# Rotary embedding of retention: how the exchanged key and query tiles are made

## The reference, cut to what matters

```
def axial_rope(x, row, col):
    def rot(xa, pos):
        half = xa.shape[-1] // 2
        freqs = ROPE_BASE ** (-jnp.arange(half, dtype=jnp.float32) / half)
        ang = pos.astype(jnp.float32)[:, None] * freqs[None, :]
        ...
        x1, x2 = xa[..., :half], xa[..., half:]
        return jnp.concatenate([x1 * cos - x2 * sin, x1 * sin + x2 * cos], axis=-1)
    h = x.shape[-1] // 2
    return jnp.concatenate([rot(x[..., :h], row), rot(x[..., h:], col)], axis=-1)
```

## Time and profile before

| | us |
|---|---|
| median of 3 runs | 2415.36 (2414.86 to 2416.98) |
| the profiled execution, its own time | 2415.04 |
| its span, first to last instruction | 2413.2 |
| PE busy | 2363.9 (98%) |
| DVE busy | 1605.0 (67%) |
| ACT busy | 930.6 (39%) |

### The profile page before, as it was taken

One profiled execution on the slowest core, in us unless ns is written; L12 is line 12 of the kernel. 1 busy time (PEld: TensorE's weight loads), 2 busy tenths in 40 slices (PEclk: granted clock), 3 DMA queues, 4 the chain that ended last, 5 costly groups with the idle time before them and its releaser, 6 DMA issues.

```text
span 2413.2 us, 33085 instructions
## 1 busy us (share of the span) xinstructions
PE 2363.9 (98%) x13282; PEld 2040.7 (85%) x13282; DVE 1605.0 (67%) x2128; ACT 930.6 (39%) x1373; POOL 125.5 (5%) x158
## 2 busy tenths in 40 slices
PE   7999999999999999999999999999999999999998
PEld 4888988998877888898889888889889896997996
DVE  7567658856368545686666786676688556678656
ACT  3422346442126322352224464224455324544343
POOL 1000001101100000010000010000010010000000
PEclk9999999999999999999999999999999999999999
DMA  9555555651233344544456575446556343675763
GB/s 298 165 163 179 189 195 162 183 183 62 55 111 88 123 131 129 159 138 151 159 173 200 175 221 162 157 162 203 185 181 183 102 129 110 216 253 185 223 203 123
DMA packets 466444, 396.33 MB, mean 164 GB/s; under 512 B 34148, under 2 KB 418292, under 8 KB 466036
## 3 DMA queue, kind: packets, MB, share of 16 engines
q1 hardware_dynamic: 450704, 386.98, 51.0%
q10 hardware_dynamic: 15588, 7.23, 1.2%
HBM read 392.99 MB, written 1.17 MB: 163 GB/s over the span
## 4 chain that ended last, share of the span: by engine, by line
PE 87%; DVE 9%; ACT 2%; issue 2%; DMA 1%; POOL 0%; SPq 0%; DVEq 0%; ACTq 0%
PE ps L1549 26%; PE ps L1551 26%; PE ps L1550 26%; DVE wl L955 2%; PE ps L1816 1%; PE ps L1892 1%; DVE st L1023 1%; PE ps L1871 1%; PE ps L1985 1%; PE ps L1596 1%; ACT wh L568 1%; PE ps L1797 1%; ACT tB L588 1%; DVE tA L1095 1%; PE ps L1631 1%
## 5 line engine op out<-in xcount | busy, mean ns | idle before, releaser
L955 DVE TENSOR_TENSOR wl<-raw,wh 128x1024 fp32r<-128x1024 f32 x560 | 681.2, 1220 | 587.0 <-ACT wh L568 585.6
L568 ACT ACTIVATE wh<-raw 128x1024 fp32r<-128x1024 f32 x560 | 592.0, 1059 | 1203.1 <-PE ps L1551 1135.3
L1549 PE MATMUL ps<-hh,wh 128*128 128x256 f32 (+1 forms) x2736 | 892.9, 326 | 8.5 <-DVE hl L1109 5.7
L1550 PE MATMUL ps<-hl,wh 128*128 128x256 f32 (+1 forms) x2736 | 885.3, 324 | 0.0
L1551 PE MATMUL ps<-hh,wl 128*128 128x256 f32 (+1 forms) x2736 | 885.1, 324 | 0.0
L1549 PEld LDWEIGHTS ps<-hh,wh 128*128 128x128 f32 x2736 | 520.9, 190 | 55.5 <-DVE hl L1109 7.6
L1550 PEld LDWEIGHTS ps<-hl,wh 128*128 128x128 f32 x2736 | 521.0, 190 | 41.7 <-issue 1.0
L1551 PEld LDWEIGHTS ps<-hh,wl 128*128 128x128 f32 x2736 | 521.0, 190 | 40.7
L970 DVE SCALAR_TENSOR_TENSOR acc<-araw,c,acc 128x1024 f32<-128x1024 f32 x210 | 258.7, 1279 | 58.0 <-DMA araw<-in_ada_w 56.1
L1549 PE MATMUL ps<-wh,stage_h_f 128*128 128x512 f32 x616 | 240.7, 391 | 2.0 <-DVE stage_l_f L1191 2.0
L1551 PE MATMUL ps<-wh,stage_l_f 128*128 128x512 f32 x616 | 239.8, 389 | 0.0
(11 more groups left out here) (187 smaller groups left out, 2277.9 us busy)
## 6 DMA issues: line engine op xcount, KB each, us to landing
raw<-in_ffa_w SPq DMA_DIRECT2D x204, 512.0 KB, 3.9
raw<-in_ffb_w SPq DMA_DIRECT2D x168, 512.0 KB, 3.8
raw<-in_mix_w_in SPq DMA_DIRECT2D x148, 512.0 KB, 4.2
araw<-in_ada_w SPq DMA_DIRECT2D x136, 512.0 KB, 5.1
raw<-in_ret_w_out SPq DMA_DIRECT2D x16, 512.0 KB, 4.5
raw<-in_na_fou_w_out SPq DMA_DIRECT2D x16, 512.0 KB, 4.0
raw<-in_mix_w_o SPq DMA_DIRECT2D x16, 512.0 KB, 3.5
raw<-in_ada_w SPq DMA_DIRECT2D x8, 512.0 KB, 5.2
```

The lines of the kernel that those rows point to most:

```text
L568: A.activation(w_home(u)[0], raw[:, s, :], ACT.Copy).then_inc(w_rounded, 1)
L955: V.tensor_tensor(low, raw[:, s, :], f(high), ALU.subtract).then_inc(w_split, 1)
L1549: T.matmul(out, a[0], b[0], start=start, stop=False)
L1550: T.matmul(out, a[0], b[1], start=False, stop=False)
```

## The change

PE's products with the swap matrix go, with the matrix, its load and their slots in PE's list. In their place ACT copies the four blocks of 32 partitions of a tile, crosswise, into a buffer (`rq2[:, j % 2, 1]`, two of them in turn). The signs move into the sine table. DVE's three operations stay, but the first reads the copied tile from SBUF instead of PSUM, and they stand two units later (after unit 12 + j instead of 10 + j). The constants are loaded one step earlier from that point on, one fewer. The bank of a unit is now n mod 4 instead of its slot mod 4.

```
+ROPE_0, ROPE_LAG = KD, 4
 def ret_slots(l):
-        if KD + 2 <= n < KD + 10:
-            out.append(("rope", j, ret_steps(l)[n - 2][0] - KD))
+        if ROPE_0 + ROPE_LAG <= n < ROPE_0 + ROPE_LAG + 8:
+            out.append(("rope", j, ret_steps(l)[n - ROPE_LAG][0] - KD))
...
 # ACT
+            def rope_swap(l, j):
+
+                n, quarter = ROPE_0 + j, DK // 4
+                t, to = kq[:, ret_steps(l)[n][0] - KD, 0:SEQ], rq2[:, j % 2, 1]
+                act.wait_ge(in_copied, 4 + in0[l] + n + 1)
+                if j >= 2:
+                    act.wait_ge(rope_done, 8 * l + j - 1)
+                for a in range(4):
+                    b = a ^ 1
+                    ins = A.copy(to[a * quarter:(a + 1) * quarter], t[b * quarter:(b + 1) * quarter])
+                ins.then_inc(rope_swapped, 1)
...
                 for j in range(RET[l]):
                     rounded(u + 4 + j)
+                    if ROPE_0 + 2 <= j < ROPE_0 + 10:
+                        rope_swap(l, j - ROPE_0 - 2)
...
 # DVE
-            def rope(l, j, k, bank):
+            def rope(l, j, k):
                 t = kq[:, k, 0:SEQ]
-                dve.wait_ge(rope_mm, 8 * l + j + 1)
-                V.tensor_tensor(rq2[:, j % 2, 0], ps[:, bank, 0:SEQ], ropeS[:], ALU.mult)
+                dve.wait_ge(rope_swapped, 8 * l + j + 1)
+                V.tensor_tensor(rq2[:, j % 2, 0], rq2[:, j % 2, 1], ropeS[:], ALU.mult)
                 link(V.tensor_tensor(t, t, ropeC[:], ALU.mult))
                 V.tensor_tensor(t, t, rq2[:, j % 2, 0], ALU.add).then_inc(rope_done, 1)
...
 # PE
-                for m, slot in enumerate(slots):
-                    if m >= 4:
-                        before = slots[m - 4]
-                        if before[0] == "unit":
-                            pe.wait_ge(in_copied, c0 + 3 + before[1] + 1)
-                        else:
-                            pe.wait_ge(rope_done, 8 * l + before[1] + 1)
-                    if slot[0] == "rope":
-                        _, j, k = slot
-                        pe.wait_ge(in_copied, c0 + 3 + KD + j + 1)
-                        T.matmul(ps[:, B[m % 4], 0:SEQ], swap[:], kq[:, k, 0:SEQ], start=True, stop=True).then_inc(rope_mm, 1)
-                        continue
-                    _, n, r, lo, hi = slot
+                for n, (r, lo, hi) in enumerate(ret_steps(l)):
+                    if n >= 4:
+                        pe.wait_ge(in_copied, c0 + 3 + n - 3)
...
-                    form_a(u + n, B[m % 4], src, hi, n0=lo)
+                    form_a(u + n, B[n % 4], src, hi, n0=lo)
...
 # constants
+        S[half * 2 * q:half * 2 * q + q] *= -1
```

More of the change, by code:

```diff
@@ L134, in trunk @@
         ident = sb("ident", [P, P])
-        swap = sb("swap", [P, P])
         ropeC = sb("ropeC", [P, SEQ])
@@ L237, in trunk @@
         rg_sig, rg_silu = sem("rg_sig"), sem("rg_silu")
-        rope_mm, rope_done = sem("rope_mm"), sem("rope_done")
+        rope_swapped, rope_done = sem("rope_swapped"), sem("rope_done")
         dec_arg, dec_exp, dec_ready = sem("dec_arg"), sem("dec_exp"), sem("dec_ready")
@@ L363, in trunk @@
         f0 = [0, len(f_items[0])]
-        N_CONST = 9
+        N_CONST = 8
         SCORE_BANKS = (0, 1, 6)
@@ L684, in tables @@
             def tables(q):
-                if HEAD <= q < HEAD + 4:
-                    dst, name = ((swap, "k_swap"), (ropeC, "k_rope_c"), (ropeS, "k_rope_s"), (wmask, "k_wmask"))[q - HEAD]
+                if HEAD <= q < HEAD + 3:
+                    dst, name = ((ropeC, "k_rope_c"), (ropeS, "k_rope_s"), (wmask, "k_wmask"))[q - HEAD]
                     act.dma_start(dst[:], io[name]).then_inc(const_in, 16)
@@ L1414, in mixer @@
                 B = in_banks(i)
-                for n, slot in enumerate(ret_slots(l)):
-                    bank = B[n % 4]
+                for slot in ret_slots(l):
                     if slot[0] == "rope":
-                        rope(l, slot[1], slot[2], bank)
+                        rope(l, slot[1], slot[2])
                         continue
                     _, n, r, lo, hi = slot
+                    bank = B[n % 4]
                     if n == 0:
@@ L1918, in mixer @@
                 u = AT["ret_in", l]
-                B, slots = in_banks(i), ret_slots(l)
+                B = in_banks(i)
                 pe.wait_ge(h_lo, pre0(i) + LT)
-                for m, slot in enumerate(slots):
-                    if m >= 4:
-                        before = slots[m - 4]
-                        if before[0] == "unit":
-                            pe.wait_ge(in_copied, c0 + 3 + before[1] + 1)
-                        else:
-                            pe.wait_ge(rope_done, 8 * l + before[1] + 1)
-                    if slot[0] == "rope":
-                        _, j, k = slot
-                        pe.wait_ge(in_copied, c0 + 3 + KD + j + 1)
-                        T.matmul(ps[:, B[m % 4], 0:SEQ], swap[:], kq[:, k, 0:SEQ], start=True, stop=True).then_inc(rope_mm, 1)
-                        continue
-                    _, n, r, lo, hi = slot
+                for n, (r, lo, hi) in enumerate(ret_steps(l)):
+                    if n >= 4:
+                        pe.wait_ge(in_copied, c0 + 3 + n - 3)
                     if n == X_UNITS:
                         pe.wait_ge(h_lo, pre0(i + 1))
-                    form_a(u + n, B[m % 4], src, hi, n0=lo)
+                    form_a(u + n, B[n % 4], src, hi, n0=lo)
                     if n == 7:
@@ L2056, in constants @@
     k = {"k_ident": np.eye(P, dtype=f32)}
-    swap = np.zeros((P, P), f32)
     C, S = np.zeros((P, SEQ), f32), np.zeros((P, SEQ), f32)
@@ L2066, in constants @@
             C[rows], S[rows] = np.cos(ang), np.sin(ang)
[L2067 to L2071, removed]
+        S[half * 2 * q:half * 2 * q + q] *= -1
+    k["k_rope_c"], k["k_rope_s"] = C, S
     d = np.arange(P)
```

## The result

The changed kernel takes 2444.89 us (median of 4 runs, 2443.34 to 2445.65), the kernel before 2415.65 in the same comparison: ratio 1.0119, 95% interval 1.0107 to 1.0130, so 29.2 us slower. The prediction was 2435.5, with a range of 2425 to 2446.

The account below looks back on a forecast made before the run. PE, busy for 98% of the span, was taken as the bound. Layer 0 +6.0, layer 1 +12.7 and clock +1.7 make 20.4 on 2415.04: 2435.5 us, range 2425 to 2446 (forecast's own 2427 to 2442).

Parts of the forecast that it names:

- The removal: PE's eight swap-matrix slots per layer, products and gaps, cost 4.68 us; at most 9.4 us in both layers.
- The ring: ACT-DVE loop from j = 2: rounding, split, copy, three rotary operations, four copies, next rounding; six turns bound.
- The turn: One pass through the ACT-DVE loop: 5.0 us, where PE needs one rounding every 2.88.
- My upper bound: Four ACT copies without overlap take 1.6 us; the forecast took 1.20.
- Layer 0: Unit 22 ends at 46.09 after the rounding of unit 10, before at 40.11: +6.0 us, net of products removed.
- The wait ahead of unit 16: PE waits 5.2 us for the rest of the context tile, which DVE does after step 13's rotary result.
- Layer 1: PE's values wait for all rotary results and start in effect at 44.2 instead of 31.47: +12.7 us, plus 1.7 clock.
- The clock: After PE's gap of over 10 us in layer 1, granted clock 0.66 for five us: 1.7 us lost, added once.
- the ring of slots hides the wait: Faster rival: only the removal counts, 2405.7 us; chance 0.08.
- The clock that keeps falling: Rival: uncovered falls in layer 0 and twice in layer 1, 1.7 us each, three to six: 2441 to 2446; chance 0.09.
- The copies that don't overlap: Copies take 1.6, a turn 5.4, twelve turns 4.8 us more: 2440; counted in the forecast's own range.

Follow-up runs that it names:

- the exchange free of charge: Changed kernel with neither swap-matrix products nor copies; DVE multiplies the unexchanged tile with the sine table: 2411.02 us, 0.9979 of the kernel before.
- the last kernel: Changed kernel with lag 2, context tile earlier on ACT and DVE, last copy ahead of last split, values' tiles reordered, later rotary wait: 2404.99 us, 0.9957.
- two kernels that open it in different ways: Changed kernel with rotary operations one unit earlier (2417.32 us), and changed kernel with four buffers instead of two for exchanged tiles (2417.47 us).
- lag 3: Changed kernel with the rotary operations of tile j after unit 11 + j instead of 12 + j on DVE: 2417.32 us, 1.0005 of the kernel before.
- four buffers: Changed kernel with four buffers instead of two for exchanged tiles, so copies of tile j wait for tile j - 4: 2417.47 us, 1.0005.
- the one with one copy: Changed kernel with one straight 128x256 copy in place of four crosswise 32x256 ones, partners not exchanged: 2429.08 us, 1.0053.
- the first four experiments: Changed kernel with rotary operations one unit earlier (2417.32 us), four buffers (2417.47), one straight copy instead of four (2429.08), or no exchange (2411.02).
- the order of the context tile: Changed kernel with rotary operations one unit earlier, context tile modulated ahead of step 12's copies, its rest on DVE at n = 13: 2410.74 us, 0.9979.
- four copies of 128x64: Changed kernel with four 128x64 copies exchanging columns on the same partitions, in place of four 32x256 ones: 2432.97 us (one run).
- straight copy: Changed kernel with the four 32x256 copies going quarter a to quarter a instead of crosswise: 2443.74 us (one run).

## Why the prediction was right, point by point

**The removal** (4.7 us a layer): right. With the exchange free of charge each stage is faster by about that, less the waits left; the last kernel has the copies and gets the whole of it. In its layer 0 the roundings after units 10 and 22 are 35.42 us apart (timeline of ACT), where the prediction had 40.11 before: 4.69 less.

```profile
452.35 1.06 ACT L570 ACTIVATE wh<-raw 128x1024 fp32r<-128x1024 f32 x1 [1.53 <-PE ps L1570]
...
487.77 1.06 ACT L570 ACTIVATE wh<-raw 128x1024 fp32r<-128x1024 f32 x1 [1.82 <-PE ps L1570]
```

The stretch of layer 1, up to the same rounding in the values as above, is 5.1 shorter. So the two stages give 9.8 of this kernel's gain. The fall of the clock of the earlier trace rows, 1.7 us, is absent from its trace, though PE's waits there are as before, so that part of the profiled execution's gain is luck.

**The ring**: right, and shown by two kernels that open it in different ways, with all copies in place. The turn was mis-sized: 5.0 predicted, 5.54 measured. The step is "Instructions of ACT overlap by 0.10 ... Four copies then take 1.20". They don't overlap here, and neither does the rounding behind them: 1.67 from the first copy to the rounding. My upper bound, no overlap at 1.6, was the true case; I took the other, and the rows of before that I used for the overlap were of instructions on the same partitions. The rest of the turn, from the rounding to the first copy, took 3.87 (1865.64 to 1869.51) where I had 3.80.

**Layer 0** (+6.0): +9.5. Six turns longer by 0.54 give 3.2, so 9.2. The other 0.3 to 0.4 are a slip of mine: I let unit 22 end 2.88 after its start, but here "end" is the rounding behind a unit. Unit 22 starts at 499.32 in the timeline of PE, and the roundings that follow 2.88 apart (508.33 after unit 24) put its end at 502.57, 3.25 later. The wait ahead of unit 16, 5.9 against 5.2, doesn't enter, since units 20 to 22 wait for ACT after it.

**Layer 1** (+12.7 and 1.7 of clock): +17.7. With the longer turns 15.9. PE's timelines show it at the product with which the second half of the first unit of the values starts, before and after:

```profile
1868.72 0.50 PE L1549 MATMUL ps<-wh,hh 128*128 128x512 f32 x1
...
1894.29 0.77 PE L1565 MATMUL ps<-wh,hh 128*128 128x512 f32 x1 [12.20 <-DVE kq L1309]
```

Counted from the rounding after unit 10, that is 34.17 and 50.22: 16.05 later. From this product to the last rounding shown, the changed kernel takes 1.69 more (15.73 against 14.04). That is the clock: PE starts again at half clock, which by the windows costs 0.35 to 1895 and 5 x 0.30 = 1.5 in the next, 1.85 in all.

**The clock**: in the two stages one fall counts, in layer 1, as put. Others came: behind unit 16 in both layers (0.62 and 0.69 from 470 to 480; 0.50 from 1865 to 1870) and in unit 21 of layer 0 (0.66 from 495 to 500). They are covered in the changed kernel, since units 20 to 22, or the values, wait for ACT and DVE in any case. Where the ring is open they are not covered, which is what my expectations for lag 3 and four buffers missed. The granted clock also fell outside the stage, in stretches that had 1.00 in the kernel before; this is in the changed kernel's windows:

```profile
2075.00:2085.00 10.00, 7.55 (x50) 0.83 0.46 135
2240.00:2250.00 10.00, 8.83 (x61) 0.83 0.44 126
```

Each is worth up to 1.7 us, and the last 1.8 of the 29.1 fall in that part. That these falls make up the 1.8 is not shown, and other traces speak against it: from the same rounding in the values to the end of the span, the kernel with four buffers takes 1.2 us more than the kernel before and the one with one copy 2.8, and neither has such a fall there, but for one at the very end that the kernel before has too. The runs of the kernel before differ by as much among themselves (2414.43 to 2417.93 beside the first four experiments), so the 1.8 stay open.

**The rivals**: that the ring of slots hides the wait needed a turn of 4.0 or less in layer 0 and 2.9 in layer 1; it was 5.54. The clock that keeps falling would have cost 1.7 us for each of three to six falls; in the stages it cost 1.7 in all, as the forecast had it, and what the two later falls cost is open. The copies that don't overlap, which the prediction put at 2440, are what came.

**The number**: the profiled execution is 8.7 us over the forecast, and outside the forecast's own range (2427 to 2442). The twelve longer turns are 6.5 of it, the end of unit 22 is 0.4, and the open part is 1.8. It lies within 2425 to 2446 because that range had room for a clock that keeps falling, which is not what used it: the mechanism was right, and that the range held is in part luck.

## What to carry to other kernels

A wait added to an in-order engine is priced by what stands ahead of the awaited result in the other engine's program, not by the length of the work it guards. If something there depends on what the waiting engine did just before, the two run in a loop, one full turn for each step, however idle both look; opening it took one number (2417.32 us instead of 2444.89), or two more buffers (2417.47). Time taken off the bounding engine shows only once what it meets next is moved too: the lag alone gave nothing over the kernel before, with the order of the context tile 5 us, and with the tail 10.9.

## What the runs showed of the hardware

ACT's instructions overlap by 0.10 us when they are on the same partitions (four copies of 128x64 end 0.69 after the first has started, and the rounding behind them starts at 0.59), and by 0.09 when one has 32 partitions and starts on the same block as the one ahead (0.97 from the rounding to the first straight copy). They don't overlap when one reads another block of 32 partitions than the one ahead (1.09 from the rounding to the first crosswise copy; 1.67 from the first of four copies to the rounding, crosswise or straight). Whether a change of the written block alone would hold an instruction, no run here shows. The Trainium skill, "VectorE: DVE Perf Modes", in "Two Vector instructions with no wait between them", says of VectorE that an instruction whose input or output starts in another quadrant of 32 partitions than the last one in that memory is held until all earlier ones have finished. The rows here agree with that for ScalarE, of which that section doesn't speak.
